# Ten row steps in the second retrieval, its key scores side by side with the queries, and convolution row steps kept out of the tap units

## What is computed

```
u = c_c * c_in
Cv = c_b * (u[t-2]*w0 + u[t-1]*w1 + u[t]*w2)          # the taps
h = LN1(alpha*x + W_out[sigmoid(g_a)*(A W_pa) + sigmoid(g_c)*(Cv W_pc)])
qy = h @ peer_w_q                                     # 8 heads x (128 + 128)
s1, s2 = qy[..., :128] @ k1.T, qy[..., 128:] @ k2.T   # key scores of the two sides
v1,i1 = top16(s1); v2,i2 = top16(s2)
cand = v1[:,None] + v2[None,:]; sc,pos = top16(cand)
eid = expert ids at pos; g = softmax(sc)
f = sum_k g_k * gelu(h . U[eid_k]) * V[eid_k]
y = LN2(alpha*h + f)
```

## Time and profile before

| what | value |
|---|---|
| three runs | 4021.99, 4020.37, 4016.74 us, median 4020.37 |
| the profiled execution | 4025.86 us, span 4024.1 us |
| PE, PEld busy | 3616.4, 3404.7 us |
| DVE, ACT, POOL busy | 2998.9, 1229.7, 1790.2 us |
| mean granted TensorE clock | 0.946 |

### The profile page before, as it was taken

The page is one execution under the profiler, slowest core; times in us unless marked ns, Lnnn a source line. Parts: engine busy times, 40 slices in busy tenths (PEclk is TensorE's granted clock), DMA queues, the critical chain, the costliest instruction groups (busy, mean ns, idle before and its releaser), DMA issues. The chain is left out here.

```text
span 4024.1 us, 64681 instructions
## 1 busy us (share of the span) xinstructions
PE 3616.4 (90%) x25095; PEld 3404.7 (85%) x25095; DVE 2998.9 (75%) x5917; ACT 1229.7 (31%) x2041; POOL 1790.2 (44%) x1364
## 2 busy tenths in 40 slices
PE   8999997998787799878549999999999999999998
PEld 8999997886675799858538899999999999999986
DVE  3434433434489588757979799999989999899997
ACT  2313313222254222124349422222222222222221
POOL 0000000000166355316769466666666666666661
PEclk9999998999898899989769999999999999999999
DMA  4122121897464587931018899999999999999996
GB/s 137 41 77 72 29 78 36 327 377 222 152 225 148 196 316 297 334 116 54 16 55 239 290 386 385 368 387 387 379 361 369 388 379 375 369 380 384 377 362 227
DMA packets 473387, 1015.56 MB, mean 252 GB/s; under 512 B 49552, under 2 KB 247824, under 8 KB 471176
## 3 DMA queue, kind: packets, MB, share of 16 engines
q0 software_dynamic: 149264, 543.49, 35.7%
q1 hardware_dynamic: 322600, 463.64, 33.2%
q10 hardware_dynamic: 1232, 4.46, 0.3%
HBM read 938.38 MB, written 126.82 MB: 265 GB/s over the span
## 5 line engine op out<-in xcount | busy, mean ns | idle before, releaser
L607 POOL DMA_INDIRECT u_row<-in_peer_u_dram,eid x512 | 731.1, 1428 | 622.2 <-DVE dots L625 496.0
L81 PE MATMUL e_ps<-coef_h,v_h 128*128 128x288 f32 x2048 | 617.7, 302 | 56.9 <-DVE v_l L2328 43.9
L613 POOL DMA_INDIRECT v_row<-in_peer_v_dram,eid x512 | 581.5, 1136 | 187.3 <-issue 155.0
L642 DVE SCALAR_TENSOR_TENSOR f_row<-v_row,g_coef,f_row 128x1024 f32<-128x1024 f32 x508 | 652.7, 1285 | 3.9 <-DMA v_row<-in_peer_v_dram,eid 2.8
L625 DVE CUSTOM_DVE_ANT_0 u_row<-u_row,h_row 128x1024 f32<-128x1024 f32 x512 | 621.8, 1215 | 5.1 <-DMA h_row<-s_h 2.8
L81 PE MATMUL e_ps<-tokens_Bh,u_h 128*128 128x288 f32 x2048 | 607.7, 297 | 8.0 <-DVE u_l L2322 7.2
L83 PE MATMUL e_ps<-coef_h,v_l 128*128 128x288 f32 x2048 | 614.0, 300 | 0.0
L82 PE MATMUL e_ps<-coef_l,v_h 128*128 128x288 f32 x2048 | 613.3, 299 | 0.0
L82 PE MATMUL e_ps<-tokens_Bl,u_h 128*128 128x288 f32 x2048 | 606.6, 296 | 0.0
L83 PE MATMUL e_ps<-tokens_Bh,u_l 128*128 128x288 f32 x2048 | 603.7, 295 | 0.0
L81 PEld LDWEIGHTS e_ps<-coef_h,v_h 128*128 128x128 f32 x2048 | 394.7, 193 | 66.4 <-DVE v_l L2328 50.4
(11 more groups left out here) (431 smaller groups left out, 8365.0 us busy)
## 6 DMA issues: line engine op xcount, KB each, us to landing
u_raw<-in_peer_uT_dram SPq DMA_DIRECT2D x128, 512.0 KB
v_raw<-in_peer_vQ_dram SPq DMA_DIRECT2D x256, 256.0 KB
s_g<-gate_block SPq DMA_DIRECT2D x9, 4096.0 KB, 16.1
x_gate<-s_g SPq DMA_DIRECT2D x64, 576.0 KB
out_o_kv_sample_dram<-in_cache_kv_w_dram SPq DMA_DIRECT2D x32, 1016.0 KB, 8.6
c_rawA<-in_conv_tiles_dram SPq DMA_DIRECT2D x40, 512.0 KB, 6.4
c_rawB<-in_conv_tiles_dram SPq DMA_DIRECT2D x40, 512.0 KB
w_raw<-in_w_in_dram SPq DMA_DIRECT2D x96, 192.0 KB
```

Of the source, the lines that this page charges most:

```text
L81: pe.matmul(out, lh, rh, start=first, stop=False)
L607: pool.indirect_dma_start(k["u_row"][:, r % RING], None, io["peer_u"][0], bass.IndirectOffsetOnAxis(ap=k["eid"][:, r:r + 1], axis=0)).then ...
L613: pool.indirect_dma_start(k["v_row"][:, v % RING], None, io["peer_v"][0], bass.IndirectOffsetOnAxis(ap=k["eid"][:, v:v + 1], axis=0)).then ...
L642: dve.scalar_tensor_tensor(out=f, in0=row, scalar=coef, in1=f, op0=ALU.mult, op1=ALU.add).then_inc(k["weighed"], 1)
```

## The change

- `conv_gates`: the weights of the row steps over the units become 2, 0, 1, 2, 2 (for LATE; EARLY has none). Of 60 steps, the units of a channel block get 2, 0, 1, 2 and 2 or 3.
- `retrieve` takes `y0`, `first_rows` = 6 and `last_rows` = 4. VectorE does six row steps ahead of `top(0)` and four between `finish` of head 6 and `finish` of head 7. GpSimd fetches three rows ahead of its first two weight splits, three after them, and four after its last look-up. ScalarE calls `row_gelus` for them.
- TensorE does queries and scores of side 0, then queries and scores of side 1. ScalarE (`sides`) copies in the same order, with the wait for `topped` in each side; GpSimd's program for a head is unchanged. VectorE waits for each side on its own.
- The retrieval's block ends without the drain of GpSimd.
- The experts start at row step 86 instead of 76, so they hold 442.

```diff
--- before.py
+++ after.py
@@ conv_gates
-    at_row = spread(y0, rows, [1] * NQ)
+    at_row = spread(y0, rows, [2, 0, 1, 2, 2] * KD)
@@ retrieve
-def retrieve(nc, io, k, half):
+def retrieve(nc, io, k, half, y0, first_rows, last_rows):
...
-        block = c.enter_context(nc.Block())
+        block = c.enter_context(nc.Block(no_gpsimd_drain=True))
@@ retrieve, scalar
-            def queries(h, more=True):
+            def sides(h, p, more=True):
                 for x in range(2):
                     for y, (a, w) in enumerate(half.chunks):
...
                     if more:
                         split_w(h + 1, x)
-
-            def scores(h, p):
-                act.wait_ge(topped, h + 1)
-                for x in range(2):
+                    act.wait_ge(topped, h + 1)
                     act.wait_ge(s_ready, h * 2 + (x + 3))
...
             for x in range(2):
                 split_w(0, x)
-            over_heads(act, lambda i, p, more: (queries(i, more), scores(i, p)),
+            row_gelus(act, k, y0, y0 + first_rows)
+            over_heads(act, sides,
                        lambda i, p: (exp(i, p), one_hot(i)))
+            row_gelus(act, k, y0 + first_rows, y0 + first_rows + last_rows)
@@ retrieve, gpsimd
             pool.wait_ge(consts, 48)
+            for r in range(y0 + RING, y0 + RING + first_rows // 2):
+                fetch_rows(pool, k, io, r)
             for x in range(2):
                 split_w(0, x)
+            for r in range(y0 + RING + first_rows // 2, y0 + RING + first_rows):
+                fetch_rows(pool, k, io, r)
             over_heads(pool, lambda i, p, more: queries(i, more), look_up)
+            for r in range(y0 + RING + first_rows, y0 + RING + first_rows + last_rows):
+                fetch_rows(pool, k, io, r)
@@ retrieve, vector
             def top(h, p):
-                dve.wait_ge(s_copied, h * 2 + 3)
-                dve.memset(tick[:], 0.0)
                 for x in range(2):
+                    dve.wait_ge(s_copied, h * 2 + (x + 2))
+                    dve.memset(tick[:], 0.0)
                     top16(lambda t, n: s1[:n, p, x, t], lambda t, n: wk[:n, x, t],
...
+            for y in range(y0, y0 + first_rows):
+                row_step(dve, k, y)
             top(0, 0)
...
             finish(HEADS - 2, 0)
+            for y in range(y0 + first_rows, y0 + first_rows + last_rows):
+                row_step(dve, k, y)
             finish(HEADS - 1, 1)
@@ program
-            phase(retrieve, LATE)
+            phase(retrieve, LATE, y0[3], 6, 4)
...
-        phase(experts, y0[3])
+        phase(experts, y0[3] + 10)
```

6 lines of the change are left out of this document (2 added, 4 removed).

## The result

The change makes the kernel slower: 4053.09 us (median of 4 runs, 4049.17 to 4056.04) against 4018.55 us (median of 4, 4015.8 to 4021.99). The ratio is 1.0085, 95% interval 1.0067 to 1.0102, so about 34.5 us. The forecast was 4018 us, the range 3994 to 4041: the time lies above both.

A forecast was written before the change was run, and what follows sets the result against it. TensorE waits for weights in the late convolution, VectorE and TensorE for each other in the experts; VectorE paces the retrieval. Convolution -17, experts -12, retrieval +24, its end +3 sum to -2: 4018 us, range 3994 to 4041.

The forecast's parts named there:

- the retrieval's: Second retrieval, to the last look-up: the new order of queries and scores costs +24 us, bounds +3 and +45.
- the start: Start of the retrieval: fetches ahead of GpSimd's weight split make TensorE begin at 1814.6 instead of 1808.0 us.
- the filling: Retrieval's heads before the first look-up: 19.6 us a head on TensorE instead of 17; first look-up at 1877.4, not 1862.5.
- the ring: Retrieval's loop: GpSimd's queue becomes a closed ring of 30.6 us a head, where VectorE needs 27.
- The convolution: Late convolution: new row-step weights remove most of TensorE's waits for the weights' low part; -17 us, bounds -8 and -21.
- 6.4 + 1.6 + 1.8: Retrieval before the first look-up: TensorE's time for each side, 9.8 us, so 19.6 us a head instead of 17.
- the slower rival: Second side's queries in the retrieval: TensorE stays at 1.2 GHz, 48 matmuls take over 8.5 us; 4043 us, chance 0.17.
- back to full pace with the second chunk: Evidence against TensorE never warming up: after the pause ahead of the retrieval's first head, full pace returned with the second chunk.
- VectorE becomes the one that waits: Retrieval's loop: look-ups come 30.6 us apart while VectorE needs 27, so VectorE waits for GpSimd.
- a VectorE wait for `looked_up`: Sign of a right forecast in the retrieval: VectorE waits for look-ups 30 us apart, GpSimd not for VectorE's release.
- The end: End of the retrieval: shared ports 2 us, queued issues about 1 us; together +3 us.
- The experts: Experts: ten row steps fewer, 2 us per activation-slot step and 0.5 per value-slot step; -12 us, bounds -5 and -24.

## Why the prediction was wrong

The term that failed is the retrieval's: +24 us were forecast up to the last look-up, and 46.0 measured. Of the 22 us between them 2.0 are the start, 9.7 the filling, 0.8 the ring's pace, and 9.5 the step from the sixth look-up to the last. The first big one failed on the clock, the last on VectorE, which was taken for the engine that waits and was slowed beside GpSimd instead.

**The convolution: right.** -16.2 against -17 in the profile, -19 alone (within its bounds of -8 and -21); TensorE's waits fell to 5.4 us in after, "some 6" was forecast. Two errors cancelled: the phase gained 19.3 us, and the branches gave back 4.1, which I had not priced, so that the total came out so close is in part luck.

**The filling: the first step that failed.** I took each side at 9.8 us, "6.4 + 1.6 + 1.8", TensorE at full pace, and gave the first look-up +14.9 in all. It was +26.6. The copies of a side's first chunk came 13.0, 11.5 and 11.4 us apart (1813.8, 1826.8, 1838.3, 1849.6). After four of the six waits for `q_l` the clock was down. The first chunk of the next side then took 4.1 to 5.1 us instead of 3.1, 4.5 us more in three sides; three groups of scores took 2.0 to 2.8 us instead of 1.5, 3 us more; and the first wait was 3.9 us and not 1.75, 2 us more. That makes up the 9.7 us that the filling took beyond the forecast. One side without a slow part took 9.9 us, so the 9.8 was right for full pace. I had this mechanism as the slower rival and looked for it in the ring only; its evidence against, "back to full pace with the second chunk", held here too, but the new order can pay for a pause at every side, where I counted one. The Trainium skill (TensorE: Matmul & The Clock Gate, Part 1) lets the level follow how busy TensorE has been recently. That spoke for the rival, and the trace agrees, with 0.50 to 0.72 in the scores behind those four waits. The rival's own condition, over 8.5 us for the 48 matmuls in the ring, was not met: the second side's 48 took 7.3 to 7.4 us there.

**The ring: right in size, wrong in what it does.** 30.6 us were forecast and 30.7 measured; the sixth look-up came 155.1 us after the first, forecast 154.3. What failed is "VectorE becomes the one that waits" and, with it, "VectorE takes its result 14.4 + 1.7 us later". I left VectorE at the 27 us a head that it "now needs", and sized the shared ports at the end of the retrieval only. In the changed kernel its heads took 35.6, 33.4, 30.6, 33.5, 27.4 and 25.8 us without a wait for a look-up, because its small operations fell beside GpSimd's and, twice, the stall of 4.2 us came on top. So it was still in the next head's top-16, and took the result 24.3 us after the start (2044.9 against 2020.65). The sign that I had set, "a VectorE wait for `looked_up`", did not come. The last look-up so came 51.7 us after the sixth instead of 42.2. By the trace of before it could have been seen: there the last is 52.1 us behind the sixth too. The sum for GpSimd's pace was right, but it was not what the end waited for.

**The start: nearly right**, +8.6 against +6.6. The difference is mostly the splits beside row steps, 5.86 for the two instead of 4.7 us. The six steps themselves were hidden, as forecast.

**The end: the mechanism right, the size under half.** 2 us were taken for the shared ports, 4.9 measured, inside the bounds of 0 and 7. Not priced: the row steps are slowed too, so VectorE itself came to the last reduction 3 us after the look-up's end. The eight issues cost nothing that shows: the gates' first GpSimd operation waited 0.41 us more for VectorE behind them.

**The experts: the test was too small.** -12 forecast for ten steps, -7.7 measured. The rule "2 us for a step in an activation slot" rested on two groups. The runs show that it is the arrangement that counts and not only the number: 12 steps moved from activation into value slots are worth some 20 us when the slots alternate (4000.5 against 3979.7) and nothing when they stand in pairs (4006.9), and four taken out of the even spread bring nothing (3979.7 against 3987.0).

**The range.** The bounds of the parts held but for one: the retrieval was bounded by +3 and +45 and came to +46.0 (8.6 + 18.0 + 19.4). What didn't hold was the choice inside them, and that the range stopped at one dear term. The half clock, VectorE's slower heads, the dearer end and the smaller gain in the experts came together, and they had a common cause only in part. With 4053.1 us the time lies even above the slow rival's 4043, which had only the clock in it.

## What to carry to other kernels

Before two steps of one engine are put side by side, ask what answers each: if the answer comes from a queue that is busy with something else, the order in batches was the overlap, and the order in pairs makes a wait per step. A short wait on TensorE can cost more than its length, so count the waits, not only their sum. An engine that never waits can still have become slower: before you name the one that sets the pace, compare the lengths of its instructions and not only its waits. Work that fits into an idle stretch of VectorE is not free beside GpSimd, in either direction; and where two engines trade waits, try the arrangement of the filler work before its amount.

## What was not expected of the hardware

- VectorE and GpSimd slow each other by more than I allowed: the new order alone made VectorE's instructions 24.8 us longer over six heads; a weighing took 3.4 to 3.9 us beside a look-up and 1.3 alone, a `CAST` of 128 x 240 elements 740 ns in the mean instead of 285. One GpSimd operation of 1.9 us per head lengthened the heads by 1.6 us, with 3.9 us of slack left.
- Waits of TensorE of 1.75 us can be enough to bring its granted clock down, to 0.66 in the window of 6 us around one of them and 0.55 in the scores behind it; but behind two of six in the filling, and behind those of 1.8 us in the ring, it stayed at 1.00, and what decides it is open. With the waits filled by matmuls that nothing reads the loop ran at 1.00.
- A stall of 4.2 to 4.4 us at the head of the second and third pass through VectorE's loop, where other kernels have 0.7, in kernels that differ from those only in the code around it.
